# Second block's attention: two row halves of a pair as one double unit in a lane of two PSUM banks, the six other units in a lane of one

## What is computed

```python
for l in range(DEPTH):                                  # 2
    h = rms_norm_2(x, norm1_g[l]); proj = h @ w_in[l]
    y_a = mla_mixer(...)     # 4 heads; q, k of 96 dims      A
    y_b = diff_mixer(...)    # 4 heads; two maps of 32 dims  B: p[0] - lam * p[1], then @ v
    y_c = swa_mixer(...)     # 4 heads of 64, window, sinks  C
    y_d = na_mixer(...)      # 4 heads of 64, rel. bias      D
    mix = concat([rms_norm_2(y_a, ..), y_b, rms_norm_2(y_c, ..), rms_norm_2(y_d, ..)])
    x = x + mix @ w_out[l]
    h = rms_norm_2(x, norm2_g[l])
    x = x + jnp.square(jax.nn.relu(h @ w_up[l])) @ w_down[l]
```

## Time and profile before

| | |
|---|---|
| median of 3 runs | 1479.4 us (1476.24 to 1483.46) |
| the profiled execution | 1481.0 us, its span 1478.8 us (2.2 us lie outside the span) |
| mean granted TensorE clock | 0.962 of full speed |
| PE / DVE / ACT busy | 1314.6 / 730.4 / 526.9 us |
| attention stage, units of layer 1 | 850.2 to 958.9 us |
| attention stage, units of layer 2 | 1174.0 to 1282.4 us |

### The profile page before, as it was taken

The page is one execution under the profiler, slowest core; times in us unless marked ns, Lnnn a source line. Parts: engine busy times, 40 slices in busy tenths (PEclk is TensorE's granted clock), DMA queues, the critical chain, the costliest instruction groups (busy, mean ns, idle before and its releaser), DMA issues. The chain is left out here.

```text
span 1478.8 us, 21544 instructions
## 1 busy us (share of the span) xinstructions
PE 1314.6 (89%) x9066; PEld 981.4 (66%) x9066; DVE 730.4 (49%) x1126; ACT 526.9 (36%) x894; POOL 50.7 (3%) x46
## 2 busy tenths in 40 slices
PE   5999998766579999976666999999999999999997
PEld 2765674433247667633432778789898878799986
DVE  1744653121146467321111777765555777764554
ACT  3535331000044354200000546654444546644343
POOL 0200000000002000000000110000000110000000
PEclk9999999888899999998887999999999999999999
DMA  9798799999977957999999714456555305455551
GB/s 353 284 334 308 280 413 421 421 421 420 399 283 275 341 200 301 421 421 421 421 393 402 179 32 172 142 156 202 186 193 173 107 3 198 143 168 189 186 198 43
DMA packets 135976, 392.10 MB, mean 265 GB/s; under 512 B 26816, under 2 KB 40128, under 8 KB 111296
## 3 DMA queue, kind: packets, MB, share of 16 engines
q1 hardware_dynamic: 132128, 389.48, 70.7%
q10 hardware_dynamic: 3744, 1.15, 0.4%
HBM read 389.45 MB, written 1.05 MB: 264 GB/s over the span
## 5 line engine op out<-in xcount | busy, mean ns | idle before, releaser
L413 DVE TENSOR_TENSOR spl<-ring,spl 128x2048 fp32r<-128x2048 f32 x65 | 149.3, 2297 | 135.7 <-ACT spl L404 135.7
L536 PEld LDWEIGHTS ps<-hh,spl 128*128 128x128 f32 x1728 | 204.1, 189 | 6.9 <-issue 5.8
L536 PE MATMUL ps<-hh,spl 128*128 128x256 f32 x1728 | 206.2, 280 | 2.8 <-DVE hh L499 2.8
L404 ACT ACTIVATE spl<-ring 128x2048 fp32r<-128x2048 f32 x66 | 126.7, 1920 | 148.3 <-PE ps L536 107.7
L2335 PE MATMUL ps<-spl,ur 128*128 128x512 f32 x768 | 176.7, 389 | 0.0
L2335 PEld LDWEIGHTS ps<-spl,ur 128*128 128x128 f32 x768 | 143.2, 188 | 29.2
L925 DVE TENSOR_TENSOR spl<-ring,spl 128x1024 fp32r<-128x1024 f32 (+2 forms) x120 | 138.4, 1175 | 24.6 <-ACT spl L916 24.2
L1337 PE MATMUL ps<-ring,ar 128*32 128x256 f32 x928 | 98.5, 443 | 57.4 <-issue 25.0
L1337 PE MATMUL ps<-spl_as_slots,ar 128*32 128x256 f32 x864 | 103.8, 479 | 45.1 <-DMA spl_as_slots<-in_w_up 29.3
L916 ACT ACTIVATE spl<-ring 128x1024 fp32r<-128x1024 f32 (+2 forms) x120 | 116.8, 1011 | 49.4 <-DMA ring<-in_w_out 11.7
L516 PE MATMUL ps<-spl,hh 128*128 128x512 f32 x480 | 117.6, 398 | 3.8 <-DVE spl L925 1.3
(11 more groups left out here) (370 smaller groups left out, 1758.5 us busy)
## 6 DMA issues: line engine op xcount, KB each, us to landing
ring<-in_w_up SPq DMA_DIRECT2D x52, 1024.0 KB, 5.3
spl_as_slots<-in_w_down SPq DMA_DIRECT2D x50, 1024.0 KB, 15.4
ring<-in_w_ada SPq DMA_DIRECT2D x48, 1024.0 KB, 7.2
spl_as_slots<-in_w_up SPq DMA_DIRECT2D x40, 1024.0 KB, 17.4
ring<-in_w_gate SPq DMA_DIRECT2D x38, 1024.0 KB, 16.8
ring<-in_w_down SPq DMA_DIRECT2D x38, 1024.0 KB, 4.9
ring<-in_w_in SPq DMA_DIRECT2D x34, 1024.0 KB, 7.5
ring<-in_w_out SPq DMA_DIRECT2D x16, 1024.0 KB, 6.9
```

Of the source, the lines that this page charges most:

```text
L404: sc.activation(t.hi, t.raw, ACT.Copy).then_inc(s_hi, 2)
L413: v.tensor_tensor(t.lo, t.raw, t.hi, ALU.subtract).then_inc(s_lo, 1)
L536: ins = pe.matmul(ps[:, banks[m // 2], (m % 2) * 256:(m % 2) * 256 + 256], le, ri, start=(kk == 0 and q == 0 and m % 2 == 0), stop=(kk == ...
```

## The change

Units that differ only in their half of the partitions (pair 0 with 1, or 2 with 3) become one double unit of four maps. Lane 0 has seven doubles and two banks (3 and 4); lane 1 has the six units left over and bank 5. The scores of a double are issued so that the two halves of the array alternate. DVE's and ACT's steps of a double are one instruction over both banks where the operation allows it (maximum, bias, copy, y), and stay two or four where a scalar differs for each map. The third lane is gone (its place in the argument list is an empty generator), and the order strings of the stage are new. PE's string has 83 digits in place of 109. A unit's products, transposes and exponentials are the same in number and size.

```diff
-         ("mix2", 0, "PE"): "4000040040001230010210310243101241234023120413242132401423421031203101213230131420023130132124030023240034201", ...
+         ("mix2", 0, "PE"): "40000400040031003030314100134034111040413113343140313401030143031310030131140101400", ...
...
-                self.b, self.units = 3 + z, UNITS[z::3]
...
+                self.b, self.units, self.n = 3 + 2 * z, units, 2 - z
...
+                self.banks = ps[:, self.b:self.b + n, :]
+                self.scores = self.banks.rearrange("p a (j n) -> p a j n", n=256)
...
+        LANES = [Lane(0, units_of(("B", 0, (0, 1)), ("B", 1, (0, 1)), ("B", 0, (2, 3)), ("A", 0, (0, 1)), ("C", 0, (0, 1)), ("D", 0, (0, 1)),
+                                  ("D", 1, (0, 1)))),
+                 Lane(1, units_of(("B", 1, (2,)), ("B", 1, (3,)), ("A", 1, (0,)), ("A", 1, (1,)), ("C", 1, (0,)), ("C", 1, (1,))))]
...
-                for j, (q, k) in enumerate(u.qk):
-                    ins = pe.matmul(ps[:, L.b, 256 * j:256 * j + 256], q, k, start=True, stop=True)
+                for j in range(2):
+                    for a in range(len(u.ps)):
+                        q, k = u.qk[a][j]
+                        ins = pe.matmul(ps[:, L.b + a, 256 * j:256 * j + 256], q, k, start=True, stop=True)
...
+                for a in range(L.n):
+                    for j in range(2):
+                        m = 2 * a + j
+                        ins = sc.activation(L.pt[:, a, j, :], src[:, a, j, :], ACT.Exp, bias=top[:, m:m + 1], scale=1.0 if masked else u.scale,
+                                            accum_out=total[:, m:m + 1])
...
-                sc.activation(L.ptT.rearrange("p a b c -> p (a b c)")[:, 0:w], ps[:, L.b, 0:w], ACT.Copy).then_inc(L.scalar, 1)
+                sc.activation(L.ptTw[:, :, 0:w], L.banks[:, :, 0:w], ACT.Copy).then_inc(L.scalar, 1)
...
-                v.wait_ge(*own_dve(v.tensor_reduce(sm[:, 0:2], src, AX.X, ALU.max)))
+                v.wait_ge(*own_dve(v.tensor_reduce(pair(top), src, AX.X, ALU.max)))
```

More of the change, by code:

```diff
@@ L373, in program @@
         a_ev, v_ev = sem("in2_scalar"), sem("in2_vector")
-        p_ln, a_ln, v_ln = ([sem(f"mix2_unit{q}_{n}") for q in range(3)] for n in ("psum", "scalar", "vector"))
+        p_ln, a_ln, v_ln = ([sem(f"mix2_unit{q}_{n}") for q in range(2)] for n in ("psum", "scalar", "vector"))
         s_r2 = sem("square_rstd")
@@ L1738, in program, with __init__ @@
-        LANES = [Lane(z) for z in range(3)]
+            def __init__(self, z, units):
+                self.b, self.units, self.n = 3 + 2 * z, units, 2 - z
+                n = self.n
+                self.sm = [st[:, 160 + 24 * z + 2 * n * q:160 + 24 * z + 2 * n * q + 2 * n] for q in range(6)]
+                pt, ptT = ((xn[:, 0, :], xn[:, 1, :]) if z == 0 else (carve(5632, 512), carve(7424, 512)))
+                self.pt = pt.rearrange("p (a j b) -> p a j b", j=2, b=256)
+                self.ptT = ptT.rearrange("p (a j b c) -> p a j b c", j=2, b=2, c=128)
+                self.ptTw = ptT.rearrange("p (a n) -> p a n", n=512)
+                self.banks = ps[:, self.b:self.b + n, :]
+                self.scores = self.banks.rearrange("p a (j n) -> p a j n", n=256)
+                self.psum, self.scalar, self.vector = p_ln[z], a_ln[z], v_ln[z]
@@ L1743, in units_done, with na_bias @@
             for L in LANES:
-                n = max(i for i, u in enumerate(L.units) if u.br == br)
-                out.append((L.vector, 3 * (len(L.units) * l + n + 1)))
-            return out
-        def na_bias(u):
-            return m2.na[u.p].rearrange("p h r c -> p h (r c)")[:, ::-1, 128 * u.i:128 * u.i + 256][:, :, ::-1]
+                n = [i for i, u in enumerate(L.units) if u.br == br]
+                if n:
+                    out.append((L.vector, 3 * (len(L.units) * l + n[-1] + 1)))
+            return out
+        def na_bias(p, i):
+            return m2.na[p].rearrange("p h r c -> p h (r c)")[:, ::-1, 128 * i:128 * i + 256][:, :, ::-1]
         OB, OD = (0, 1, 2, 6), (3, 4, 5, 7)
@@ L1862, in pe_units @@
                 pe.wait_ge(L.scalar, 2 * at + 2)
-                for j, c in enumerate(u.vs):
-                    for kt in range(2):
-                        ins = pe.matmul(ps[:, L.b, 64 * j:64 * j + 64], L.ptT[:, j, kt, :], m2.v[:, kt, c:c + 64], start=(kt == 0), stop=(kt == 1))
+                for a, vs in enumerate(u.vs):
+                    for j, c in enumerate(vs):
+                        for kt in range(2):
+                            ins = pe.matmul(ps[:, L.b + a, 64 * j:64 * j + 64], L.ptT[:, a, j, kt, :], m2.v[:, kt, c:c + 64], start=(kt == 0),
+                                            stop=(kt == 1))
                 ins.then_inc(L.psum, 1)
@@ L1953, in pe_mix2 @@
                 pe_spin(pe, 6, 2)
-            steps(ORDER["mix2", l, "PE"], pe_main2(pe, g, l), *(pe_units(pe, l, L) for L in LANES), pe_misc2(pe, l))
+            steps(ORDER["mix2", l, "PE"], pe_main2(pe, g, l), pe_units(pe, l, LANES[0]), iter(()), pe_units(pe, l, LANES[1]), pe_misc2(pe, l))
         def act_main2(sc, l):
@@ L2079, in act_mix2 @@
             act_hT(sc, g, PR(f"n1{l}"), last, 1)
-            steps(ORDER["mix2", l, "ACT"], act_split(sc, last), *(act_units(sc, l, L) for L in LANES), act_misc2(sc, l), act_main2(sc, l))
+            steps(ORDER["mix2", l, "ACT"], act_split(sc, last), act_units(sc, l, LANES[0]), iter(()), act_units(sc, l, LANES[1]), act_misc2(sc, l), act_main2(sc, l))
             for c in range(2):
@@ L2142, in dve_units @@
                 at = len(L.units) * l + n
[L2143 removed]
+                src, scale = L.scores, u.scale
                 if u.br == "D" and L.units[n - 1].br != "D":
@@ L2274, in dve_mix2 @@
             dve_hT(v, g, PR(f"n1{l}"), last, 1)
-            steps(ORDER["mix2", l, "DVE"], dve_split(v, last), *(dve_units(v, l, L) for L in LANES), dve_misc2(v, l), dve_main2(v, l))
+            steps(ORDER["mix2", l, "DVE"], dve_split(v, last), dve_units(v, l, LANES[0]), iter(()), dve_units(v, l, LANES[1]), dve_misc2(v, l), dve_main2(v, l))
             v.wait_ge(s_used, T["out2", l, 2].m + 1)
```

116 lines of the change are left out of this document (65 added, 51 removed), and 4 rows, old and new, of the table ORDER.

## The result

| | before | after |
|---|---|---|
| median of 13 runs | 1480.12 us (1476.24 to 1484.06) | 1486.44 us (1483.54 to 1493.06) |
| ratio | | 1.0046 (95%: 1.0033 to 1.0060) |
| profiled execution, span | 1481.0, 1478.8 us | 1489.4, 1487.2 us |
| mean granted TensorE clock | 0.962 | 0.952 |

The forecast was 1479.7 us, +0.3. The profiled execution of after is 2.9 us above its own median, that of before 0.9; so 8.4 us between the two traces stand for 6.3 between the medians. Of all runs in this document one was slow (1709.35 us at a granted clock of 0.736, of the change once more), and medians and ratios leave it out.

A forecast was written before the change was run, and what follows sets the result against it. The prediction took PE to bound the stage: 9.6 us of saved work against net 9.9 us of new waits gave +0.3 us, 1481.3 on the profiled execution and 1479.7 us as median, with a range of 1471 to 1489.

The forecast's parts named there:

- What PE saves: B, C and D doubles in both layers: opposite halves stream at once, saving 5.1 + 4.5 = 9.6 us of PE work.
- the accidental pair: Kernel before, at 851.24: two units of opposite halves happen to follow each other, eight records through in 1.06 us.
- The sign that I had named: Both layers' stages: PE's busy time down by some 4 to 5 us in each would show the forecast right.
- The third rival: Doubles' scores: halves overlap at three of seven seams only, five slots instead of four, giving 1482.3 us; chance 0.05.
- New waits, net 9.9: Both layers' stages: 12.3 us of newly shown waits less 2.4 us of old waits that go.
- item 1: Where B ends and A begins, both layers: waits of 1.35 for a copy, 1.1 before the next S; 3.0 a layer.
- Item 2: Layer 1, second B double: a copy of 0.60 with 0.05 of way, and a y of 0.57; 1.2 us.
- Item 4: Layer 2, C and D: copies 0.15 each, a C unit's P 0.9, y 0.65, last copy 0.65; 2.5 us.
- Item 3: Layer 1, both D doubles: copy 0.25, y before S 0.65, last P 1.7; sum 2.6 us.
- Saved work and new waits within some 6 us of each other: The forecast's own case over both layers: saving and waits nearly cancel, +0.3 us; chance 0.67.
- the savings: Faster rival, both layers: PE waits no more than the 2 us of now, 9.6 us come off, 1469.8; chance 0.14.
- the double lane: Slower rival: seven doubles in one lane form a chain that becomes the bound, 15 us more, 1495; chance 0.14.

The follow-up runs named there:

- the change once more: The unaltered changed kernel run a second time, on one chip with a later version: 1485.55 us, 1.0031 against the kernel before.
- The dummies: Changed kernel plus three dummy matmuls ahead of V of lane 1's first A unit (both layers) and layer 1's third output tile: 1482.62 us, 1.0005.
- halves in turn: Changed kernel with a double's scores issued as four records of one half, then four of the other, instead of two by two: 1485.12 us, 1.0031.
- the full-clock trace: Changed kernel with layer 1's end in layer 2's order and three dummy matmuls ahead of lane 1's first A unit's V, both layers: 1480.21 us, 1.0000.
- both places relaid: Changed kernel with layer 1's end in layer 2's order; between B and A, ACT's copy and norm precede the splits, DVE's y precedes B's scaling: 1483.11 us, 1.0013.
- all three queues: Changed kernel with PE's, ACT's and DVE's orders laid anew at the place between B and A, both layers: 1493.98 us, 1.0089.

## Why the prediction was right, and where it wasn't

The forecast of no change over 0.5% and its range held; the sum of +0.3 us was 6.0 us short. That the range held is in part luck: its upper side, 9 us of splits in the way of other units, was priced for something that didn't happen, and it left room for a cost that I hadn't thought of. Term by term:

- *What PE saves*, 9.6 us: right, 9.7 at full clock. The row of the accidental pair was worth the whole term. The sign that I had named, PE's busy time down by 4 to 5 us in each stage, shows only there (4.3 and 5.4); in the trace of the change it is 1.4 up and 2.5 down. The third rival isn't borne out: with the halves one after the other a double would have cost 1.7 us, and both orders took 1.06. The Trainium skill, "TensorE: Matmul & The Clock Gate", Part 3, states that matmuls start and end strictly in queue order; by these 1.06 us the traces of this case don't agree.
- *New waits, net 9.9*: 10.9, right as a sum, but for two reasons that cancel. In item 1, "PE waits 1.35" for the copy was 2.6, since the splits ahead of it wait 1.3 for their DMA; the "1.1 more" for the next S was 0.1, since V's delay gave DVE the time to be done. Per layer 2.6 + 0.4 + 0.1 = 3.1 against 3.0.
- *Item 2*, 0.65 and 0.57: 0.7 and 0.4. *Item 4*, 0.9 and twice 0.65: 0.8, 0.65 and 0.68. Both right.
- *Item 3*, layer 1's end: the 0.25 and 0.65 were 0.3 and 0.5. But "the last P has only 3.3 ahead of it ... 1.7" was the wrong place: the output tile ahead of that P waited 3.1 us for C's turned y, and P then not at all. I followed a unit's round through DVE and not what DVE's queue holds for the main line behind the same masked sums. This is what I had said would prove me wrong, a wait over 1 us at a place not named.
- *What failed* is a term that isn't in the sum at all: "Saved work and new waits within some 6 us of each other" takes each record at one duration. In the trace of the change PE's records took 10.0 us more than at full clock, some 7 of them at the three waits of 2.6 to 3.1 us. The other 2.9 are at the second B double, where before has 1.4. The dummies, which leave every wait as it is, gave 6 us back by the ratios (1.0046 to 1.0005); within a chip, the version with dummies was faster than its nearest neighbour without by 2.5, 2.9 and 4.5 us in the medians of the three chips (the change against its halves in turn; the other two pairs differ in an order as well).
- *The rivals*: the savings didn't come through; the double lane wasn't the bound either, B doubles waited 0.7 and 0.4 us at most.

The sum by what was measured: 9.7 saved, 10.9 of waits, 10.0 − 1.4 = 8.6 of clock, so +9.8 in the traces' stretches, as the windows have it. This is one execution, and a slow one of its kind. The later runs of the change and of its twin with the halves in turn have a ratio of 1.0031 both, 4.6 us.

Open: why the trace of the change is 2.9 us above its median; and why a stretch at the lower clock around 880 to 888, where the versions hardly differ, comes in most traces, before's too, and not in the two with layer 1's end relaid and A's units as in the change (PEclk 1.00). Those orders differ from the change's only behind this place, so they can't be the reason. Nor are the small waits there (0.7 and 0.4) enough: the full-clock trace has both of them, and before's has the slow stretch right behind 12 us in which PE never waited (868 to 880; the last records ahead of it are products on 32 rows, L1906). No order was found in which the A place has neither wait nor dummies. The chain leads there to the weights' DMA of 5.2 us behind A's v; that it sets the place is read from the chain, and an earlier release of that buffer wasn't tried.

## What to carry to other kernels

Fewer and larger units shorten PE's work but take away the small pieces that cover each other's rounds; count the new waits, and then add what PE's clock may take on top: in the two traces of the change three waits of 8.3 and 8.0 us together came with some 7 and 6 us of longer records. Don't count on short waits to be spared. Pieces of 0.4 to 1.1 us at the A place came with the lower clock in both runs that had nothing longer there and no dummy, though those at the end of layer 2 in the change (0.8, 0.65 and 0.7) didn't. When a step is late, follow its engine's queue upward past the instruction ahead of it to what that one waits for: twice here (splits behind a DMA, a turned y behind masked sums) the price was in the second link. Where a wait can't be removed, dummy matmuls inside it are a cheap cure, and a good test of whether the wait or its clock is the cost. And compare more than one trace: the same kernel lost 10.0 us to the clock in one and 7.2 in the other.

## What the runs showed of the hardware

- At each of the change's three waits of 2.6 us or more PE's granted clock fell to the lower level (0.52 to 0.72 in the windows), with twelve records of a half tile in 5.46 instead of 3.02 us. Three dummy matmuls (six records, 2.74 us) in the wait kept it at 1.00 behind every wait that had them.
- A long wait isn't needed for it: waits of 0.69, 1.05 and 0.46 us (both places relaid) and of 0.7, 0.4 and 1.1 us (all three queues) had it as well, in the change once more it came ahead of the long wait at layer 1's end, and in the kernel before at 880 it came behind no wait at all.
- Scores on opposite halves of the array overlap fully in either queue order (1.06 us for eight records, two by two or four by four); on the same half they take 1.92.
- DVE's maximum over 1024 elements took 1.22 us against 0.69 for 512, as I had taken from a subtraction of that width.
